# A bound of four on the row sets that GpSimd has under way in a PEER step

## What is computed

```
h = x + W_o [ sigmoid(g_a) * (A(xn) W_a) + sigmoid(g_b) * (B(xn) W_b) ]     # two attentions
y = RMSNorm_final( h + PEER(RMSNorm(h)) )

def expert_block(args):                     # PEER: xb (128, 1024), eb and gb (128, 128)
    u = jnp.take(u_tab, eb, axis=0)         # one row of 4 KB per position and expert
    act = jax.nn.gelu(jnp.einsum('cd,ced->ce', xb, u))
    v = jnp.take(v_tab, eb, axis=0)
    return jnp.einsum('ce,ced->cd', gb * act, v)
```

## Time and profile before

| | |
|---|---|
| median of three runs | 1905.93 us |
| profiled execution, span | 2029.6 us |
| PE, DVE, POOL, ACT busy in it | 1467.7, 1202.8, 1067.7, 380.8 us |
| moved by DMA | 706.43 MB, mean 348 GB/s |
| of it by GpSimd's queue | 612.40 MB |
| requests for v rows in WR (line 660) | 432, 427.0 us busy, 988 ns each |
| requests for u rows in XS (line 660) | 258, 269.2 us busy, 1043 ns each |

### The profile page before, as it was taken

The page is one execution under the profiler, slowest core; times in us unless marked ns, Lnnn a source line. Parts: engine busy times, 40 slices in busy tenths (PEclk is TensorE's granted clock), DMA queues, the critical chain, the costliest instruction groups (busy, mean ns, idle before and its releaser), DMA issues.

```text
span 2029.6 us, 18882 instructions
## 1 busy us (share of the span) xinstructions
PE 1467.7 (72%) x5470; PEld 670.5 (33%) x5470; DVE 1202.8 (59%) x3335; ACT 380.8 (19%) x923; POOL 1067.7 (53%) x1082
## 2 busy tenths in 40 slices
PE   8999998756886687768996555555555666676657
PEld 5444443443443333322442222222222233221111
DVE  1034352585577567667666776677676777687541
ACT  2113441222222222111111111211111212111101
POOL 3020000264575566766566666666666666666674
PEclk9999999976897888778997877777777777776778
DMA  9999998697999799999999989999999999998997
GB/s 329 359 310 365 362 318 304 199 323 260 389 388 362 274 375 343 396 397 375 396 364 403 376 332 344 342 365 361 368 352 368 347 352 357 354 361 332 369 369 284
DMA packets 226136, 706.43 MB, mean 348 GB/s; under 512 B 21153, under 2 KB 46657, under 8 KB 226009
## 3 DMA queue, kind: packets, MB, share of 16 engines
q0 software_dynamic: 166912, 612.40, 80.5%
q1 hardware_dynamic: 59120, 92.82, 13.2%
HBM read 700.65 MB, written 72.61 MB: 381 GB/s over the span
## 4 chain that ended last, share of the span: by engine, by line
PE 26%; DVE 23%; issue 19%; DMA 11%; POOL 9%; another core or an unknown queue 8%; ACT 1%; SPq 1%; DVEq 0%; POOLq 0%; ACTq 0%
PE bank L1059 7%; PE bank L947 4%; DVE XS L1463 4%; POOL WR L660 4%; DVE GT L1463 3%; DMA arena<-in_peer_u_dram,e_all 3%; PE bank L1175 3%; POOL XS L660 2%; DMA WR<-in_peer_v_dram,arena 2%; DVE arena L1463 2%; PE bank L1076 2%; PE bank L1196 2%; PE bank L1154 2%; DMA WR<-in_w_in_dram 2%
## 5 line engine op out<-in xcount | busy, mean ns | idle before, releaser
L1059 PE MATMUL bank<-WR,arena 128*64 128x512 f32 x1728 | 536.1, 724 | 189.8 <-issue 82.1
L660 POOL DMA_INDIRECT WR<-in_peer_v_dram,arena x432 | 427.0, 988 | 301.0 <-issue 145.4
L660 POOL DMA_INDIRECT XS<-in_peer_u_dram,e_all x258 | 269.2, 1043 | 225.7 <-DVE XS L1463 77.4
L1059 PEld LDWEIGHTS bank<-WR,arena 128*64 128x64 f32 x1728 | 146.8, 163 | 520.2 <-issue 470.2
L1463 DVE SCALAR_TENSOR_TENSOR XS<-XS,bank 128x1024 f32<-128x1024 f32 x144 | 171.2, 1218 | 41.3 <-DMA XS<-in_peer_u_dram,e_all 38.8
L1463 DVE SCALAR_TENSOR_TENSOR GT<-GT,bank 128x1024 f32<-128x1024 f32 x126 | 150.0, 1218 | 59.8 <-DMA GT<-in_peer_u_dram,e_all 45.3
L1463 DVE SCALAR_TENSOR_TENSOR XS<-XS,GT 128x1024 f32<-128x1024 f32 x114 | 137.4, 1225 | 80.1 <-DMA XS<-in_peer_u_dram,e_all 65.6
L660 POOL DMA_INDIRECT GT<-in_peer_u_dram,e_all x126 | 123.1, 977 | 52.3 <-issue 33.9
L660 POOL DMA_INDIRECT arena<-in_peer_u_dram,e_all x128 | 127.4, 995 | 42.1 <-issue 37.8
L754 ACT ACTIVATE XS<-bank 128x256 f32<-128x256 f32 (+1 forms) x90 | 36.2, 405 | 469.1 <-remote 267.7
L1076 PE MATMUL bank<-WR,XS 128*128 128x512 f32 x256 | 116.0, 607 | 0.4 <-ACT arena L754 0.4
(11 more groups left out here) (234 smaller groups left out, 2122.9 us busy)
## 6 DMA issues: line engine op xcount, KB each, us to landing
out_dram<-in_cache_a_k_dram POOLq DMA_DIRECT2D x8, 4064.0 KB, 54.6
out_dram<-in_cache_a_v_dram POOLq DMA_DIRECT2D x8, 4064.0 KB, 55.4
WR<-in_w_in_dram SPq DMA_DIRECT2D x8, 2048.0 KB, 25.7
GT<-in_w_peer_q_dram SPq DMA_DIRECT2D x14, 1024.0 KB
WR<-in_w_out_dram SPq DMA_DIRECT2D x6, 2048.0 KB
WR<-in_peer_v_dram,arena POOLq DMA_INDIRECT x432
WR<-in_w_branch_a_dram SPq DMA_DIRECT2D x6, 1024.0 KB, 7.6
WR<-in_w_branch_b_dram SPq DMA_DIRECT2D x6, 1024.0 KB, 9.7
```

What stands on the lines that cost most here:

```text
L660: nc.gpsimd.indirect_dma_start(dst, None, table, bass.IndirectOffsetOnAxis(ap=idx, axis=0))\
L1059: last = nc.tensor.matmul(b[c][R * j:R * j + R, :], diag[p // QUAD % 4][:, s % 4, :], V[V_AT[s]][:, c * CHUNK:(c + 1) * CHUNK], start=Fals ...
```

## The change

A list `asked_for` holds, for u and v together and in the order of the requests, the landing semaphore of each row set and the value it has once that set has landed. Ahead of each request GpSimd now waits for the entry four back. So at most four row sets, the one about to be asked for among them, are between request and landing. The wait comes after those for the buffer. A `nop` that stood ahead of every u and every second v now stands ahead of every v as well. Nothing else is changed, on no other engine.

```diff
--- before.py
+++ after.py
@@ -41,6 +41,7 @@
 
 
 G = 2
+FLIGHT = 4
 R = P // G
 NHEADS = TILES * PH
 UQ = (TILES * SLOTS + DEC) // QUAD
@@ -660,6 +661,14 @@
                 nc.gpsimd.indirect_dma_start(dst, None, table, bass.IndirectOffsetOnAxis(ap=idx, axis=0))\
                     .then_inc(landed, 16)
 
+            asked_for = []
+
+            def in_flight(landed, value):
+
+                if len(asked_for) >= FLIGHT:
+                    pool.wait_ge(*asked_for[-FLIGHT])
+                asked_for.append((landed, value))
+
             def expert(s):
                 p = prompt_slot(s)
                 if p is None:
@@ -691,6 +700,7 @@
                 elif U_AT[s] == 7:
                     emptied(pool, "post", TILES - 1, 0)
                     emptied(pool, "post", TILES - 1, 1)
+                in_flight(u_landed[U_AT[s]], 16 * U_FILL[s])
                 pool.nop(nofuse=True)
                 gather(U[U_AT[s]], pu, expert(s), u_landed[U_AT[s]])
 
@@ -708,8 +718,8 @@
                     pool.wait_ge(S["held"], 2)
                 elif V_AT[s] == 11 and V_OLD[s] is None:
                     pool.wait_ge(y_out[1], 16)
-                if s % G == 0:
-                    pool.nop(nofuse=True)
+                in_flight(v_landed[V_AT[s]], 16 * V_FILL[s])
+                pool.nop(nofuse=True)
                 gather(V[V_AT[s]], pv, expert_v(s), v_landed[V_AT[s]])
 
             for pieces in PLAN:
```

## The result

| | before | after |
|---|---|---|
| median | 1903.63 us (4 runs, 1897.69 to 1910.49) | 2197.53 us (4 runs, 2190.2 to 2205.5) |
| ratio | | 1.155, 95% interval 1.151 to 1.159 |
| span of the profiled execution | 2029.6 us | 2188.4 us |

The prediction was 1998 us, range 1920 to 2095. Slower was right, the size was not: +294 us where it had +92.

The account below looks back on a forecast made before the run. Memory was taken to bound the kernel from 376 us on (DMA share 0.95 and 0.94). To the 1905.93 us median it added +72 us late and +20 us early, +92 in all: 1998 us, range 1920 to 2095.

Parts of the forecast that it names:

- the early term: 432 requests up to 1110 us at 1.50 us each: 648 us against 580, mostly absorbed by buffer waits, +20 us kept.
- The bound binds, and by a round of landing and wake: On GpSimd's queue, each request waits for the fourth before it; four take one round of wake, request and landing, 6.01 us.
- Wake 0.77 us: On GpSimd, time from a freed buffer to the start of the waiting request, taken for the new wait too: 0.77 us.
- Landing 5.24 us, hence 1.50 us per request: From request start to landing with two requests just ahead: 5.24 us; with the wake a round of 6.01 us, 1.50 per request.
- "long-run" rival: Landings on GpSimd's queue stay at the long run's 6.40 us under the bound, 1.79 us per request: 2121 us; chance 0.15.
- Waits for buffers absorb half of the late loss: From 1110 to 1990 us, GpSimd's 134 us of buffer waits absorb half: between +5 and +139 us, +72 us kept.
- This is a stretch fed by memory: From 376 us on, DMA share 0.95 and 0.94 at 354 and 355 GB/s, no compute engine above 74%: memory sets the pace.
- The 124 us between the profiled execution and the median: Whole span: profiled execution 124 us longer than the 1905.93 us median, stretch unknown; the +92 us was added to the median unchanged.
- The page of the Trainium skill: For GpSimd's requests: 2.0 us plus bytes over 436 GB/s, landing in 3.2 us, round about 4 us, so the bound never binds.
- Not binding: Rival: at 1.30 us per request, late needs 767 of 880 us, early 562 of 734: 1906 us, within 1%; chance 0.14.
- Faster: Rival: early, weights and u rows land sooner with a shorter GpSimd queue, halving VectorE's 106 us waits: 1853 us; chance 0.08.
- All of it shows: Rival: 1.79 us per request, late +176 us even with every wait absorbed, early +39: 2121 us; chance 0.15.

Follow-up runs that it names:

- late_only: The changed kernel with the bound of four only from request 440 on, against the kernel before (2021.21 us on that chip): 2127.15 us, ratio 1.055.
- half_free: The kernel before, without a bound, each request moving 2 KB rows instead of 4 KB, on a chip where before takes 2024.95 us: 1999.69 us.
- early_only: The changed kernel with the bound of four only for the first 440 requests, against the kernel before (2021.21 us on that chip): 2097.06 us, ratio 1.038.

## Why the prediction was wrong

The direction and the mechanism were right. What failed is the size of three terms of the sum: the landing with four under way (5.24 us for 5.8), the early term (+20 us for +76), and the time before against which the late requests were set (1.49 us each, with 134 us of waits as room, for 1.31 and hardly any). Of the 202 us that the sum lacked, 76 show on the kind of chip that it was read from (+168 there for +92) and 126 come from the kernel before being faster where it was timed.

- **The bound binds, and by a round of landing and wake.** Right: the rows of after show it request by request, and the runs with two to six under way.
- **Wake 0.77 us.** Right: 0.74.
- **Landing 5.24 us, hence 1.50 us per request.** This step failed. 5.24 came from the earlier trace rows, a third request with two ahead of it: that is three under way, and FLIGHT = 3 has 5.2 us in the mean. With four it is 5.79, and 6.53 / 4 = 1.63 us. The row isn't a clean landing either: it ends in "issue" after 0.22 us, so VectorE had other work until 1365.65 and 5.24 us is only an upper bound for that set. The prediction spoke of three under way; they are three others and the one that is being asked for. The missing 0.13 us is 590 x 0.13 = 77 us late. The "long-run" rival took 6.40 us and 1.79 us per request, as far above 1.65 as 1.50 is below; that its total came closer is in part luck.
- **Early the same landing as late.** Failed: the landing there is 6.63 us and a request 1.86 us, not 1.50. SyncE's weight loads cross there; that they lengthen the landing is likely, but no run leaves them out. The earlier trace rows said that landings get long there; they went into a rival and not into the early term. At 1.50 us the term was 648 us against 734 and looked absorbed (+20 kept). It measured +76, and on the 1903 kind it is about +99 by pace.
- **Waits for buffers absorb half of the late loss.** Failed in three ways. The 134 us were not waits for buffers in the main: in the request rows behind the earlier trace rows, 37 us beyond the gaps end with an engine that frees a buffer, 69 us are "remote" and 26 us "issue", the stalls of that execution. On the kind of chip that was profiled everything short of 1.49 us is absorbed, but 1.63 x 590 = 962 us is 82 us more than the 880 even so; `late_only` measured +106 where the prediction had +72. On the kind that was timed there are 29 us of such waits and not 134, and late the pace goes from 1.31 to 1.65.
- **"This is a stretch fed by memory."** Failed for the late stretch that was read: `half_free` keeps its pace there at half the bytes and a share of 0.62. It fits the executions on the 1903 kind, at a share of 1.02 and a flat 409 GB/s, though no run there halves the bytes.
- **The 124 us between the profiled execution and the median, "carried over as it is".** This is the largest failure (126 of the 202 us, as above). No row said where they lie, and the sum was then made in the very stage where most of them lie: 355 GB/s at a share of 0.94 in one, 407 at 1.02 in the other. The trace had a sign of it: a span 6% above the median, with stalls named "issue" and "remote" on every engine. With 1.31 us as the pace before, the same round at 1.50 us would have given 590 x 0.19 = +112 us late with nothing to absorb it; with the right round it is +201.
- **The page of the Trainium skill** ("DMA: Bandwidth & Descriptors", section "Anatomy of one DMA — SWDGE (gpsimd) path": an estimated 3.2 us for a row set) was set aside rightly: the shortest landing in the 134 cases is 4.18 us, and two under way have 4.7 in the mean.
- **Rivals.** Not binding is refuted for four; at six it is true within 0.5%. Faster is refuted: the early stretch is slower (`early_only`), and VectorE's waits for u rows there grow from 106 us to over 209. *All of it shows* at 2121 us was the right side and still 77 us short, since it kept the absorption of the execution it was read from.
- **The signs.** DMA share 0.91 and 320 GB/s (below 0.94 and 355): right. VectorE's late waits 165.6 + 138.9 us in the two largest rows (over 100): right. Requests 1.4 to 1.6 us apart: missed, 1.65. Landings 5 to 5.5 us: missed, 5.8. Waits for buffers down to 60 us: missed, nearly none are left.

## What to carry to other kernels

A bound on transfers under way costs little as long as (landing + wake) / bound stays under the time per request that the kernel has without it, 1.31 us here on full engines. Count the request that is being made among those under way, and read the landing from a place with just as many, in a row where the consumer was waiting for it. In this kernel each further set lengthens the round by less than the 1.31 us, so a short queue gives bandwidth away, and eight or none give no more than six to within 0.5%. When the profiled execution is some per cent longer than the median, find the stage where it is longer before any wait in that stage is counted as room: get its rate (GB/s, share) and ask whether the median fits another rate.

## What the chips showed that was not expected

- The same kernel takes 1903 us on some chips and 2021 to 2025 on others. On the latter all compute engines stall late with nothing the profile shows (matmuls 2.12 us apart), at half the traffic and with light work too, but not where a request takes 1.65 us. What stalls them, and whether it belongs to the chip, stays open.
- The sixteen full DMA engines move 409 GB/s of 4 KB rows for one core. Six row sets of 512 KB under way give 397, four give 321.
- A row set lands after 4.7, 5.2, 5.8 and 6.0 us with two to five under way. GpSimd goes on 0.74 us after VectorE has seen the same landing, as after a freed buffer (0.77).
